# A decoder kernel whose first attention scores take k from SBUF instead of from a DRAM scratch, with two buffer changes in the second mixer and a 192-byte column buffer

## The chip, the core and the metric

The kernel runs on one core of a Trainium2 chip. The metric is the device time of one execution in microseconds (us), taken as the median of several runs. The engines are PE (TensorE, matmuls), DVE (VectorE), ACT (ScalarE), POOL (GpSimd) and SP (SyncE, which here issues DMAs). Matmul operands are float32 values split in a high and a low part, so each product is three matmul passes (L342 to L344), and every split costs one ACT cast (the high part) and one DVE subtraction (the low part).

## The reference, cut

A two-layer decoder on 512 tokens of width 1024, 16 heads of 64. Layer 0 has block-sparse (MoBA) attention between two SwiGLU blocks, layer 1 a dilated sliding-window attention with three branches that reads shared keys and values.

```python
for layer in range(DEPTH):
    if layer == N_A_LAYERS:                       # shared keys and values of three branches
        kv_bands = shared_kv_bands(modulate(rms_norm(x, kv_norm_g), ...), kv_w, cos, sin)
    x = x + 0.5 * gate0 * swiglu(modulate(rms_norm(x, g0), ...), w_gate, w_up, w_down)
    h = modulate(rms_norm(x, g1), ...)
    y = moba_mixer(h, w_qkv, w_o, cos, sin) if layer < N_A_LAYERS else dilated_mixer(h, w_q, w_o, kv_bands, cos, sin)
    x = x + gate1 * y
    x = x + 0.5 * gate2 * swiglu(modulate(rms_norm(x, g2), ...), w_gate, w_up, w_down)
return rms_norm(x, final_g)
```

Both mixers rotate q and k by position (`apply_rope`) before the scores.

## The kernel before

The residual stream `x`, the normed input `h_hi`/`h_lo` and two slots of weights (`w_raw`, `w_hi`, `w_lo`) lie in SBUF for the whole program. The program is a chain of phases: ffn0, mixA, woA, ffn1, kv, ffn2, mixB, woB, ffn3. Weights come in units of 512 KB that alternate between the two slots: SP loads a unit (`w_dma`, L327), ACT casts it (L333), DVE subtracts (L337), PE multiplies. The order on each engine is written out by hand, engine by engine, and semaphores tie the engines together; no scheduler moves anything.

**A mixer.** The 16 heads are worked in four groups of four. Group g's projections (pairs of 128 columns: in mixA pair 0 is q, pair 1 is k, pair 2 is v; in mixB pairs 0 to 2 are the q of the three branches) run while group g-1 is attended. Group 0 has nothing to hide behind. A pair of results goes from PSUM through DVE (`rope_multiply` L1430, or `late_read` L1017 for the very first pair) and POOL (`rope_add`, L1442 and L1446) into `rotated`; ACT casts it into a staging buffer (`rot_high`, L1454), DVE subtracts (`rot_low`, L1459), and POOL stores the 1 MB in a DRAM scratch (`rot_store`, L1466). `rope_add` holds all four heads of a group in rows of 32 per head and half. SP reads one head at a time back into the layout that the scores need (`load_k`, `load_q`, L1623; `load_v`, L1651): eight DMAs of 64 KB for a head's k in mixA, four for its q.

**What sets the order around the change.** SP's queue is in order. In group 0 of mixA it does: q of head 0 (waits for q's store), k of head 0 (waits for k's store), weight unit 9, v of head 0 (waits for v's store), weight unit 10, then k of head 1 (waits for the first score), unit 11, q of head 1, v of head 1. PE does units 0 to 9 of its weights in part, and then `score(a, s)` (L738, L739): steps s = 0 to 3 belong to head 0, step 4 begins head 1. `weigh_v` (L767, L768) is the product with v, two steps behind.

**Staging buffers.** `rot_st` is the one staging buffer; only the first pair of a mixer uses another one, `rot_late`, which lies on rows 3 to 6 of `att`. So in mixB, group 0, the cast of pair 2 into `rot_st` waits until the store of pair 1 out of `rot_st` has landed (`q_stored`). Behind that cast stands ACT's cast of weight unit 8, and behind DVE's `rot_low` of pair 2 stands the subtraction of unit 8. The third branch of the first head is copied straight from the staging buffer to `q_st` (L1665, four DMAs of 64 KB between SBUF rows), and the first score waits for these (`q_direct`).

**PSUM banks in mixB.** One unit is one tile of 128 columns and one bank. Group 0 uses the banks `FIRST_BANKS = (0, 1, 2, 3, 1, 7)` for its six tiles, later groups bank `unit % 3`. Tile 4 of group 0 lies in bank 1, and so tile 1 of group 1 (the program's unit 7, in bank 1) has to wait until DVE has read pair 2 of group 0 out.

Of the kernel before, what the change touches and what calls it, by code (L numbers as in the profile page):

```python
# [26 lines left out]
F32 = mybir.dt.float32  # L27
# [114 lines left out]
LATE_ROWS = (6, 7)  # L142
FIRST_BANKS = (0, 1, 2, 3, 1, 7)


def build(nc, x_t, c_col, ada_first, ada, ada_bias, gains, gate_up, down, mixa_w, kv_w, mixb_w, cos_t, sin_t,
          mask_a, mask_b, ident_in, out):
    with ExitStack() as ctx:  # L148
# [28 lines left out]
        shift_hl = sb(ctx, "shift_hl", [P, KT, 2], F32R)  # L177
        shift_out = sb(ctx, "shift_out", [P, 16])[:, 0:2]
        idle = sb(ctx, "idle", [P, S], BF16)
# [487 lines left out]
        def pe_mixer(pe, name):  # L667
# [9 lines left out]
            def substep(g, n):  # L677


                pair, k = n // KT, n % KT  # L680
                unit = n // 4
                first = isinstance(g, int) and g == 0
                follows = first and n < 2 * KT
                if n % 4 == 0:
                    pe.wait_ge(w_lo_done[unit % 2], g * 6 + u0 + unit - unit % 2 + 2)
                if is_a:
                    bank = mixa_bank(g, pair)
                    if k == 0:

                        pe.wait_ge(pair_free, g * 3 + p0 + pair + 1)  # L690
                    if follows:
                        pe.wait_ge(h_lo_done, h0 + k + 1)
                    if pair == 2:
                        mm = pe_k_tile_v(bank, unit % 2, k % 4, k, KT - 1)
                    else:
                        mm = pe_k_tile(bank, unit % 2, k % 4, h_hi, h_lo, k, KT - 1)
                else:
                    if n % 4 == 0:


                        pe.wait_ge(pair_free, g * 3 + p0 + pair + (1 if unit in (0, 2, 4) or first else 2))
                        if first and unit == 5:
                            pe.wait_ge(mod_ready, ADA_BLOCKS)
                    for j in range(2):
                        kt = 2 * (n % 4) + j
                        cols = slice(kt * P, (kt + 1) * P)
                        if follows:
                            pe.wait_ge(h_lo_done, h0 + kt + 1)
                        mm = three_passes(ps[:, FIRST_BANKS[unit] if first else unit % 3, :], w_hi[:, unit % 2, cols],
                                          w_lo[:, unit % 2, cols], h_hi[:, kt, :], h_lo[:, kt, :],  # L710
                                          kt == 0, kt == KT - 1)
                if n % 4 == 3:
                    mm.then_inc(unit_used, 1)
                elif n > 20 - 1 and not is_a and isinstance(g, int) and g == G - 1:
                    mm.then_inc(h_read, 1)
# [703 lines left out]

        rot_late = att[:, 3:7, :].bitcast(F32R).rearrange("p (a h) t -> p a h t", a=2)  # L1420

# [26 lines left out]

        def rot_high(act, n, busy, busy_n, late=False):

            act.wait_ge(rope_done, n * 2 + 2)
            if busy is not None:
                act.wait_ge(busy, busy_n)
            nc.scalar.copy((rot_late if late else rot_st[:])[:, 0], rotated[:]).then_inc(rot_hi_done, 1)  # L1454

        def rot_low(dve, n, late=False):
            st = rot_late if late else rot_st[:]
            dve.wait_ge(rot_hi_done, n + 1)
            nc.vector.tensor_tensor(st[:, 1], rotated[:], st[:, 0].bitcast(F32),  # L1459
                                    ALU.subtract).then_inc(rot_lo_done, 1)  # L1460

        def rot_store(pool, n, dst, dst_sem, late=False):
            st = rot_late if late else rot_st[:]
            pool.wait_ge(rot_lo_done, n + 1)
# [172 lines left out]

        def load_k(sp, layer, a, j):
            if j == 0:
                sp.wait_ge(k_stored, (a + 1) * 16 if layer == "A" else 16 * 16)  # L1640
# [13 lines left out]
        def load_q(sp, layer, a, j):  # L1654
            if layer == "B" and j == 0:
# [6 lines left out]
                for part in range(2):  # L1662
                    for half in range(2):
                        row = 64 * part + 32 * half
                        sp.dma_start(q_st[row:row + 32, 0, 2, :].bitcast(F32),  # L1665
                                     rot_st[0:32, part, half, :].bitcast(F32)).then_inc(q_direct, 16)
                return
# [69 lines left out]
        def act_mixer(act, name):  # L1737
# [5 lines left out]
            def rot(g, pair):  # L1743
                first = isinstance(g, int) and g == 0
                if first and pair < 2:
                    rot_high(act, rope0 + pair, None, 0, pair == 0)
                    return
                if is_a:
                    n, busy, busy_n = g * 2 + pair, (k_stored, q_stored)[pair], g * 16 + 16 * pair
# [171 lines left out]
        def dve_mixer(dve, name, g_block, col_n, stored):  # L1921
# [53 lines left out]
            def group(g, a, gemm, attend, early):  # L1975
# [4 lines left out]
                if not attend:  # L1980
                    for pair in range(3):
                        if pair == 0:
# [7 lines left out]
                            split(5)  # L1990
                            rot_low(dve, rot_n(g, 0), True)
                            continue
# [6 lines left out]
                        if pair == 1 or not is_a:  # L1999
                            rot_low(dve, rot_n(g, pair))  # L2000
                    split(8)
# [52 lines left out]
        def pool_mixer(pool, name):  # L2054
# [4 lines left out]
            def group(g, last=False):  # L2059
                for pair in range(3):  # L2060
# [10 lines left out]
                    if not is_a:  # L2071
                        if pair == 2:
                            pool.wait_ge(q_direct, g * 64 + 64)
                        rot_store(pool, n, dram_q["B"][g, pair], q_stored, pair == 0 and isinstance(g, int) and g == 0)
                    elif pair == 0:
                        rot_store(pool, n, dram_q["A"][g, 0], q_stored, isinstance(g, int) and g == 0)
                    else:
# [285 lines left out]
```

## Time and profile before

| | |
|---|---|
| median of 3 runs | 2497.1 us (2494.9 to 2497.17) |
| the profiled execution | 2495.63 us, span 2493.9 us |
| PE busy | 2448.9 us (98%) |
| DVE, ACT, POOL busy | 1376.2, 869.2 and 141.7 us |
| mean granted PE clock | 0.996 |
| mixA from its first scores | about 463 to 640 us |
| mixB from its first scores | about 1773 to 2100 us |

Times below are us from the start of the span. In the views an engine's idle time stands in brackets before the instruction that ended it, with what released it. The view by windows gives the granted PE clock of a stretch as a share of full speed (0.50 is 1.2 GHz, 1.00 is 2.4 GHz) and the busy share of the DMA engines. "To landing" is the time from a DMA's issue to the arrival of its last byte.

### The profile page before, as it was taken

What the parts mean: (1) busy time and instruction counts of PE and PEld (TensorE: products, weight loads), DVE (VectorE), ACT (ScalarE), POOL (GpSimd) and SP (SyncE); (2) the same over time, 40 slices, a digit from 0 to 9 for tenths busy, and PEclk for the clock granted to TensorE, in tenths of its full rate; (3) what the DMA queues carried; (4) which work ended last, traced back from release to release, by engine and by line L of the source; (5) the groups of instructions that cost most, each with busy time, mean ns of one, the idle gap of its engine ahead of it and who ended that gap; (6) DMA issues with size and microseconds to landing.
All of it is one profiled execution on the core that took longest, in us unless ns stands there. A gap on an engine that the chain in (4) does not pass through costs nothing. (4 is left out here: it accounts for less than half of the span.)

```text
span 2493.9 us, 33238 instructions
## 1 busy us (share of the span) xinstructions
PE 2448.9 (98%) x11992; PEld 2024.9 (81%) x11997; DVE 1376.2 (55%) x2105; ACT 869.2 (35%) x1230; POOL 141.7 (6%) x128
## 2 busy tenths in 40 slices
PE   9999999999999999999999999999999999999998
PEld 6888888888778888888888888888888887888886
DVE  7555446677675554465544555446667667433333
ACT  3222224345443332233333333223444444333321
POOL 0000000212000000011211000000211110000000
PEclk9999999999999999999999999999999999999999
DMA  6656532655446654335557666435887973222332
GB/s 245 196 188 194 163 118 92 209 192 179 139 155 191 192 179 133 103 114 207 179 183 246 188 189 192 132 118 143 249 223 214 241 218 97 92 93 93 101 93 84
DMA packets 135715, 408.79 MB, mean 164 GB/s; under 512 B 17088, under 2 KB 17472, under 8 KB 135616
## 3 DMA queue, kind: packets, MB, share of 16 engines
q1 hardware_dynamic: 122560, 357.16, 47.1%
q0 software_dynamic: 13056, 50.33, 5.2%
q8 instruction: 60, 0.98, 0.2%
q14 instruction: 39, 0.32, 0.0%
HBM read 353.95 MB, written 52.43 MB: 163 GB/s over the span
## 5 line engine op out<-in xcount | busy, mean ns | idle before, releaser
L337 DVE TENSOR_TENSOR w_lo<-w_raw,w_hi 128x1024 fp32r<-128x1024 f32 (+2 forms) x386 | 469.9, 1218 | 615.5 <-ACT w_hi L333 615.2
L342 PE MATMUL ps<-h_hi,w_hi 128*128 128x512 f32 x1872 | 745.3, 398 | 8.9 <-DVE w_lo L337 4.1
L344 PE MATMUL ps<-h_hi,w_lo 128*128 128x512 f32 x1872 | 732.2, 391 | 0.0
L343 PE MATMUL ps<-h_lo,w_hi 128*128 128x512 f32 x1872 | 730.9, 390 | 0.0
L333 ACT CAST w_hi<-w_raw 128x1024 fp32r<-128x1024 f32 (+2 forms) x388 | 395.5, 1019 | 765.5 <-PE ps L344 753.5
L342 PEld LDWEIGHTS ps<-h_hi,w_hi 128*128 128x128 f32 x1872 | 353.1, 189 | 83.7 <-DVE w_lo L337 8.9
L344 PEld LDWEIGHTS ps<-h_hi,w_lo 128*128 128x128 f32 x1872 | 352.4, 188 | 75.4
L343 PEld LDWEIGHTS ps<-h_lo,w_hi 128*128 128x128 f32 x1872 | 353.3, 189 | 67.1 <-issue 0.2
L342 PE MATMUL ps<-act_hi,w_hi 128*128 128x512 f32 x704 | 278.8, 396 | 0.2 <-DVE w_lo L337 0.2
L344 PE MATMUL ps<-act_hi,w_lo 128*128 128x512 f32 x704 | 277.8, 395 | 0.0
L343 PE MATMUL ps<-act_lo,w_hi 128*128 128x512 f32 x704 | 277.8, 395 | 0.0
L1328 DVE TENSOR_TENSOR prod<-ps,silu_g 128x512 f32<-128x512 f32 x86 | 59.5, 692 | 259.2 <-ACT silu_g L1286 259.2
L886 DVE SCALAR_TENSOR_TENSOR ada_acc<-ada_raw,c_act,ada_acc 128x1024 f32<-128x1024 f32 x126 | 161.2, 1279 | 0.7
L342 PEld LDWEIGHTS ps<-act_hi,w_hi 128*128 128x128 f32 x704 | 132.5, 188 | 34.1 <-issue 3.6
L344 PEld LDWEIGHTS ps<-act_hi,w_lo 128*128 128x128 f32 x704 | 132.5, 188 | 31.1
L343 PEld LDWEIGHTS ps<-act_lo,w_hi 128*128 128x128 f32 x704 | 132.6, 188 | 30.7
L1766 ACT CAST pt_hi<-ps 128x768 fp32r<-128x768 f32 (+4 forms) x128 | 78.5, 614 | 216.1 <-PE ps L748 215.9
L1286 ACT ACTIVATE silu_g<-ps 128x512 f32<-128x512 f32 x86 | 51.6, 600 | 252.3 <-PE ps L344 252.0
L1956 DVE TENSOR_TENSOR pt_lo<-ps,pt_hi 128x768 fp32r<-128x768 f32 (+4 forms) x128 | 92.4, 722 | 81.9 <-ACT pt_hi L1766 80.9
L767 PE MATMUL ps<-v_st,pt_hi 128*128 128x128 f32 x544 | 129.8, 278 | 5.9 <-DVE o_rows L1950 5.9
L768 PE MATMUL ps<-v_st,pt_lo 128*128 128x128 f32 x544 | 128.1, 275 | 0.0
L1442 POOL TENSOR_TENSOR rotated<-tmp 128x512 f32<-128x512 f32 x32 | 44.7, 1398 | 1446.5 <-DVE tmp L1017 1240.6
(162 smaller groups left out, 2808.1 us busy)
## 6 DMA issues: line engine op xcount, KB each, us to landing
w_raw<-gate_up SPq DMA_DIRECT2D x176, 512.0 KB, 3.7
ada_raw<-ada SPq DMA_DIRECT2D x144, 512.0 KB, 4.5
w_raw<-down SPq DMA_DIRECT2D x80, 512.0 KB, 3.6
w_raw<-kv_w SPq DMA_DIRECT2D x48, 512.0 KB, 3.6
w_raw<-mixa_w SPq DMA_DIRECT2D x34, 512.0 KB, 3.9
w_raw<-mixb_w SPq DMA_DIRECT2D x34, 512.0 KB, 5.6
kb<-rot_st POOLq DMA_DIRECT2D x12, 1024.0 KB, 5.0
k_hi<-kb SPq DMA_DIRECT2D x64, 192.0 KB, 4.8
```

The lines of the kernel that those rows point to most:

```text
L333: nc.scalar.copy(w_hi[:, slot, 0:n], w_raw[:, slot, 0:n]).then_inc(w_hi_done, 1)
L337: eng.tensor_tensor(w_lo[:, slot, 0:n], w_raw[:, slot, 0:n], w_hi[:, slot, 0:n].bitcast(F32), ALU.subtract).then_inc(w_lo_done[slot], 2)
L342: nc.tensor.matmul(out_ap, l_hi, r_hi, start=start, stop=False, skip_group_check=skip)
L343: nc.tensor.matmul(out_ap, l_hi, r_lo, start=False, stop=False, skip_group_check=skip)
L344: return nc.tensor.matmul(out_ap, l_lo, r_hi, start=False, stop=stop, skip_group_check=skip)
L767: nc.tensor.matmul(o_ps, pt_hi[:, s % 2, cols], v_both, start=n == 0, stop=False)
L768: mm = nc.tensor.matmul(o_ps, pt_lo[:, s % 2, cols], v_both, start=False, stop=n == n_last)
L886: nc.vector.scalar_tensor_tensor(out=ada_acc[:], in0=ada_raw[:, slot, :], scalar=c_act[:, k:k + 1], in1=ada_acc[:], op0=ALU.mult, op1=ALU. ...
L1286: nc.scalar.activation(silu_g[:, b, :], ps[:, 2 * b, :], ACT.Silu).then_inc(silu_done, 1)
L1328: nc.vector.tensor_tensor(prod[:, b, :], ps[:, 2 * b + 1, :], silu_g[:, b, :], ALU.mult).then_inc(pair_free, 1)
L1766: nc.scalar.copy(pt_hi[:, s % 2, 0:w], pt_ps[:, 0:w]).then_inc(pt_hi_done, 1)
L1956: nc.vector.tensor_tensor(pt_lo[:, s % 2, 0:w], pt_ps[:, 0:w], pt_hi[:, s % 2, 0:w].bitcast(F32), ALU.subtract).then_inc(pt_lo_done, 1)
```

## The change

Three edits, and a fourth of one number.

1. **mixA, head 0 of group 0: k on chip.** `load_k` for this head no longer waits for k's store in DRAM but for `rot_lo_done`, and copies the same eight pieces from rows 0 to 31 of `rot_st`. The store to DRAM stays, since heads 1 to 3 are read from it. ACT's next write of `rot_st` (group 1, pair 0) waits in addition for the eight copies.
2. **mixB, pair 2 of group 0** is staged in `att` rows 0 to 3 (`ROT_LATE = (0, None, 1)`), pair 0 in `att` rows 4 to 7 instead of 3 to 6. The cast of pair 2 doesn't wait for `q_stored` any more.
3. **mixB, tile 4 of group 0** goes to bank 4, after the row of factors that lay there has been copied (`rb_kept_done`). Tile 1 of group 1 waits for pair 1 of group 0 to be read out and no longer for pair 2.
4. `shift_out` takes 192 bytes of each partition instead of 64. Every buffer allocated behind it (those of the FFN, kv and mixer phases: `act_hi`, `act_lo`, `rot_st`, `k_hi`, `att` and so on) moves up by 128 bytes: `act_hi` starts at byte 106624 instead of 106496. `x`, `h_hi`, `h_lo` and the weight slots stay.

```diff
-FIRST_BANKS = (0, 1, 2, 3, 1, 7)
+FIRST_BANKS = (0, 1, 2, 3, 4, 7)
+ROT_LATE = (0, None, 1)
...
-        shift_out = sb(ctx, "shift_out", [P, 16])[:, 0:2]
+        shift_out = sb(ctx, "shift_out", [P, 48])[:, 0:2]
...
+                second = isinstance(g, int) and g == 1 and n < KT
...
-                        pe.wait_ge(pair_free, g * 3 + p0 + pair + (1 if unit in (0, 2, 4) or first else 2))
+                        pe.wait_ge(pair_free, g * 3 + p0 + pair + (1 if unit in (0, 2, 4) or first or second else 2))
+                        if first and unit == 4:
+                            pe.wait_ge(rb_kept_done, LATE.index("mixB") + 1)
...
-        rot_late = att[:, 3:7, :].bitcast(F32R).rearrange("p (a h) t -> p a h t", a=2)
+        def rot_buffer(late):
+
+            if late is None:
+                return rot_st[:]
+            return att[:, 4 - 4 * late:8 - 4 * late, :].bitcast(F32R).rearrange("p (a h) t -> p a h t", a=2)
...
         def load_k(sp, layer, a, j):
+            if layer == "A" and isinstance(a, int) and a == 0 and j == 0:
+
+                sp.wait_ge(rot_lo_done, rope_before("mixA") // 2 + 2)
+                for copy in range(2):
+                    for part, tile in enumerate((k_hi, k_lo)):
+                        for half in range(2):
+                            row = 64 * copy + 32 * half
+                            sp.dma_start(tile[row:row + 32, 0, 0, :].bitcast(F32),
+                                         rot_st[0:32, part, half, :].bitcast(F32)).then_inc(k_landed, 16)
+                return
...
-                if first and pair < 2:
-                    rot_high(act, rope0 + pair, None, 0, pair == 0)
+                if first and pair < 2 or first and not is_a:
+                    rot_high(act, rope0 + pair, None, 0, ROT_LATE[pair])
                     return
+                if is_a and isinstance(g, int) and g == 1 and pair == 0:
+                    act.wait_ge(k_landed, 128)
```

**SP in mixA, group 0**, from the last weight unit before the scores to the k of head 1. Before:

```order
L1623 DMA q_st<-qa 32x512 [waits q_stored]
L1623 DMA q_st<-qa 32x512 x3
L1623 DMA k_hi<-ka 32x512 [waits k_stored]
L1623 DMA k_hi<-ka 32x512
L1623 DMA k_lo<-ka 32x512 x2
L1623 DMA k_hi<-ka 32x512 x2
L1623 DMA k_lo<-ka 32x512 x2
L327 DMA w_raw<-mixa_w 128x1024 [waits w_lo_done1]
L1651 DMA v_st<-va 128x512 [waits v_stored]
L327 DMA w_raw<-mixa_w 128x1024 [waits w_lo_done0]
L1623 DMA k_hi<-ka 32x512 [waits s_done]
```

and now:

```order
L1631 DMA q_st<-qa 32x512 [waits q_stored]
L1631 DMA q_st<-qa 32x512 x3
L1654 DMA k_hi<-rot_st 32x512 [waits rot_lo_done]
L1654 DMA k_hi<-rot_st 32x512
L1654 DMA k_lo<-rot_st 32x512 x2
L1654 DMA k_hi<-rot_st 32x512 x2
L1654 DMA k_lo<-rot_st 32x512 x2
L328 DMA w_raw<-mixa_w 128x1024 [waits w_lo_done1]
L1669 DMA v_st<-va 128x512 [waits v_stored]
L328 DMA w_raw<-mixa_w 128x1024 [waits w_lo_done0]
L1631 DMA k_hi<-ka 32x512 [waits s_done]
```

The eight pieces keep their place in the queue; their source and the semaphore of the first of them are other ones.

**ACT in mixB, group 0**, the casts of pairs 0, 1 and 2 with the weight units between them. Before:

```order
L1454 CAST att<-rotated 128x1024 [waits rope_done]
L333 CAST w_hi<-w_raw 128x1024 [waits unit_used,w_landed0]
L1454 CAST rot_st<-rotated 128x1024 [waits rope_done]
L333 CAST w_hi<-w_raw 128x1024 [waits unit_used,w_landed1]
L1454 CAST rot_st<-rotated 128x1024 [waits q_stored,rope_done]
L333 CAST w_hi<-w_raw 128x1024 [waits unit_used,w_landed0]
```

and now:

```order
L1462 CAST att<-rotated 128x1024 [waits rope_done]
L334 CAST w_hi<-w_raw 128x1024 [waits unit_used,w_landed0]
L1462 CAST rot_st<-rotated 128x1024 [waits rope_done]
L334 CAST w_hi<-w_raw 128x1024 [waits unit_used,w_landed1]
L1462 CAST att<-rotated 128x1024 [waits rope_done]
L334 CAST w_hi<-w_raw 128x1024 [waits unit_used,w_landed0]
```

The third cast of rotated rows writes `att` and has lost the wait for the store. On no engine has an instruction been added, taken away or moved past another.

## Rows read from the trace of the kernel before

**Rows 1.** Waits of PE over the whole span: us in total, times, longest
```profile
PE ps L738 <- DMA k_lo<-ka: 4.4, 1, 4.4
```
**Rows 2.** Timeline of PE in mixA: start us, us, instruction, idle before
```profile
458.13 0.39 PE L344 MATMUL ps<-h_hi,w_lo 128*128 128x512 f32 x1
462.88 0.47 PE L738 MATMUL ps<-k_hi,q_st 128*128 128x128 f32 x1 [4.36 <-DMA k_lo<-ka]
...
472.29 0.22 PE L767 MATMUL ps<-v_st,pt_hi 128*128 128x128 f32 x1
...
476.49 0.27 PE L738 MATMUL ps<-k_hi,q_st 128*128 128x128 f32 x1
```
**Rows 3.** Windows: us, busy (x) of PE, PEld, DVE, ACT, POOL, PEclk, DMA share, GB/s
```profile
461.70:468.60 6.90, 5.72 (x16) 4.66 (x17) 1.87 (x5) 1.54 (x3) 1.99 (x2) 0.51 0.85 265
632.40:635.90 3.50, 3.50 (x10) 2.46 (x10) 2.17 (x6) 2.33 (x5) 0.00 (x0) 0.51 0.53 143
1766.00:1773.00 7.00, 4.61 (x20) 3.31 (x19) 4.75 (x6) 3.28 (x3) 0.00 (x0) 1.00 0.45 122
```
**Rows 4.** Timelines of DVE, POOL and SP's queue in mixA, group 0
```profile
449.76 1.23 DVE L1459 TENSOR_TENSOR rot_st<-rotated,rot_st 128x1024 fp32r<-128x1024 f32 x1 [3.52 <-ACT rot_st L1454]
...
451.60 0.77 POOL L1466 DMA_DIRECT2D ka<-rot_st  x1 [2.95 <-DVE rot_st L1459]
453.92 0.75 POOL L1492 DMA_DIRECT2D va<-v_out  x1 [1.56 <-DVE v_out L1484]
...
448.36 1.73 SPq L1623 DMA_DIRECT2D q_st<-qa  x4
457.83 0.78 SPq L1623 DMA_DIRECT2D k_hi<-ka  x2
...
461.92 0.42 SPq L1651 DMA_DIRECT2D v_st<-va  x1
...
463.60 0.82 SPq L1623 DMA_DIRECT2D k_hi<-ka  x2
...
468.85 1.82 SPq L1623 DMA_DIRECT2D q_st<-qa  x4
```
**Rows 5.** DMA issues (KB each, us to landing) and landing of L1665's copies
```profile
va<-v_out POOLq DMA_DIRECT2D x1, 1024.0 KB, 6.4
...
q_st<-qa SPq DMA_DIRECT2D x2, 64.0 KB, 2.9
...
DMA to landing us min/median/max: 2.0/3.2/3.8
```
**Rows 6.** DMA queue q0 from 453 to 455 us: packets, MB, share of 16 engines
```profile
q0 software_dynamic: 196, 0.80, 98.7%
```
**Rows 7.** Timeline of PE in mixB, group 1's tiles 1 and 2, first score
```profile
1762.03 0.47 PE L342 MATMUL ps<-h_hi,w_hi 128*128 128x512 f32 x1 [1.61 <-DVE tmp L1430]
...
1770.14 0.50 PE L342 MATMUL ps<-h_hi,w_hi 128*128 128x512 f32 x1 [2.39 <-DVE w_lo L337]
...
1773.02 0.47 PE L738 MATMUL ps<-k_hi,q_st 128*128 128x512 f32 x1
```
**Rows 8.** Timelines of DVE, POOL, ACT and SP's queue there; a DMA issue at 1752.3
```profile
1758.27 1.22 DVE L337 TENSOR_TENSOR w_lo<-w_raw,w_hi 128x1024 fp32r<-128x1024 f32 x1 [1.26 <-ACT w_hi L333]
...
1763.22 1.29 POOL L1446 TENSOR_TENSOR rotated<-tmp 128x512 f32<-128x512 f32 x1
...
1766.65 1.05 ACT L1454 CAST rot_st<-rotated 128x1024 fp32r<-128x1024 f32 x1 [8.48 <-DMA qb<-rot_st]
...
1766.59 1.74 SPq L1623 DMA_DIRECT2D q_st<-qb  x4
1768.98 2.50 SPq L1665 DMA_DIRECT2D q_st<-rot_st  x4
...
w_raw<-mixb_w SPq DMA_DIRECT2D x1, 512.0 KB, 11.4
```
**Rows 9.** The page's costliest groups: busy, mean ns, idle before
```profile
L342 PE MATMUL ps<-h_hi,w_hi 128*128 128x512 f32 x1872 | 745.3, 398 | 8.9 <-DVE w_lo L337 4.1
...
L342 PE MATMUL ps<-act_hi,w_hi 128*128 128x512 f32 x704 | 278.8, 396 | 0.2 <-DVE w_lo L337 0.2
```

More of the change, by code:

```diff
@@ L1447, in rope_add, with rot_high @@
                                     ALU.add).then_inc(rope_done, 1)
-        def rot_high(act, n, busy, busy_n, late=False):
+        def rot_high(act, n, busy, busy_n, late=None):
             act.wait_ge(rope_done, n * 2 + 2)
@@ L1453, in rot_high, with rot_low @@
                 act.wait_ge(busy, busy_n)
-            nc.scalar.copy((rot_late if late else rot_st[:])[:, 0], rotated[:]).then_inc(rot_hi_done, 1)
-        def rot_low(dve, n, late=False):
-            st = rot_late if late else rot_st[:]
+            nc.scalar.copy(rot_buffer(late)[:, 0], rotated[:]).then_inc(rot_hi_done, 1)
+        def rot_low(dve, n, late=None):
+            st = rot_buffer(late)
             dve.wait_ge(rot_hi_done, n + 1)
@@ L1460, in rot_low, with rot_store @@
                                     ALU.subtract).then_inc(rot_lo_done, 1)
-        def rot_store(pool, n, dst, dst_sem, late=False):
-            st = rot_late if late else rot_st[:]
+        def rot_store(pool, n, dst, dst_sem, late=None):
+            st = rot_buffer(late)
             pool.wait_ge(rot_lo_done, n + 1)
@@ L1664, in load_q @@
                         row = 64 * part + 32 * half
+                        src = rot_buffer(ROT_LATE[2] if isinstance(a, int) and a == 0 else None)
                         sp.dma_start(q_st[row:row + 32, 0, 2, :].bitcast(F32),
-                                     rot_st[0:32, part, half, :].bitcast(F32)).then_inc(q_direct, 16)
+                                     src[0:32, part, half, :].bitcast(F32)).then_inc(q_direct, 16)
                 return
@@ L1990, in group @@
                             split(5)
-                            rot_low(dve, rot_n(g, 0), True)
+                            rot_low(dve, rot_n(g, 0), ROT_LATE[0])
                             continue
@@ L1999, in group @@
                         if pair == 1 or not is_a:
-                            rot_low(dve, rot_n(g, pair))
+                            rot_low(dve, rot_n(g, pair), ROT_LATE[pair])
                     split(8)
@@ L2073, in group @@
                             pool.wait_ge(q_direct, g * 64 + 64)
-                        rot_store(pool, n, dram_q["B"][g, pair], q_stored, pair == 0 and isinstance(g, int) and g == 0)
+                        rot_store(pool, n, dram_q["B"][g, pair], q_stored,
+                                  ROT_LATE[pair] if isinstance(g, int) and g == 0 else None)
                     elif pair == 0:
-                        rot_store(pool, n, dram_q["A"][g, 0], q_stored, isinstance(g, int) and g == 0)
+                        rot_store(pool, n, dram_q["A"][g, 0], q_stored,
+                                  ROT_LATE[0] if isinstance(g, int) and g == 0 else None)
                     else:
```

## The prediction

> **What bounds the kernel now.** I read the list of PE's waits first. PE is busy nearly everywhere, so only its gaps, and stretches in which it is granted half its clock, can be won. The largest single wait is the first score of mixA, for k to come back from DRAM [rows 1]. PE's timeline puts it in place: the last matmul before it ends at 458.13 + 0.39 = 458.5, the score starts at 462.88 [rows 2]. The windows then show that the gap costs more than its length: from 461.7 to 468.6 the granted clock is 0.51, the lower level of 1.2 GHz, with 5.72 us of PE work in it, which at the full clock is half as long, 2.8 us less [rows 3]. In mixB two gaps stand before the first score: 1.61 us for DVE's reading of pair 2 and 2.39 us for weight unit 8 [rows 7]. I then read the queues that feed these places, SP's above all [rows 4, 8], because a wait that goes only helps until the next thing that is late.
>
> **Edit 1, k on chip.** Removed: the way through DRAM. DVE ends `rot_low` of k at 449.76 + 1.23 = 451.0, SP has issued q by 448.36 + 1.73 = 450.1, yet k's first load goes out at 457.83, when the store has landed [rows 4]. Now the first copy goes out at 451.0. The nearest price of such a copy is L1665's, the same size from the same buffer: four take 2.50 us to issue, 0.63 us each [rows 8]. The eighth starts at 451.0 + 7 x 0.63 = 455.4. These copies land in 2.0 to 3.8 us, median 3.2 [rows 5]; since the two stores fill the DMA engines just then (98.7%, rows 6) I take the median: 458.6, bounds 457.4 and 459.2. PE is ready at 458.5. So the wait falls from 4.4 to 0.1 us (0 to 0.7), a gain of 4.3 us, and with no gap the 2.8 us of clock come back too: 7.1 us at the first steps.
>
> **What is late next.** The SP queue. Behind k stand unit 9, then v of head 0, which waits for v's store. Before, that store landed at 453.92 + 6.4 = 460.3 [rows 4, 5], and SP came to v only at 461.92, so nobody waited. Now SP is there at 456.5 and waits. The store itself gets later: 0.5 MB of copies and the 0.5 MB of unit 9 now move while both stores are under way. At the rate of [rows 6], 0.80 MB in 2 us, this 1 MB is worth 2.5 us of all engines; the first two copies find them free, so I take 2.0: v's store lands at 462.3, bounds 460.3 (no delay) and 462.8. The Trainium skill says the same of the mechanism (DMA: Bandwidth & Descriptors, Issuing engines are not separate DMA queues): DMAs of SP and POOL interleave on the same 16 DMA engines.
>
> From 462.3 the queue runs on: v and unit 10 take 0.9, k of head 1 starts at 463.2 (before 463.60) and takes 3.6 us as before, unit 11 takes 0.4, q of head 1 starts at 467.2 (before 468.85), its last piece 1.4 later, and lands 2.9 us after that [rows 4, 5]: 471.5. PE wants it for the first score of head 1, before at 476.49, now 7.1 earlier, 469.4. It waits 2.1 us. The gain left is 476.49 - 471.5 = 5.0 us; 4.5 with the store at 462.8, and the full 7.0 with the store undelayed. v for the first `weigh_v` (472.29, now 465.2) is on the same delay and its wait lies inside this one. Behind that score SP waits for PE again and all that follows keeps its distance.
>
> One correction for the median. How long the clock stays low varies: the other low stretch behind a gap, 632.4 to 635.9, holds 3.50 us of work and so costs 1.75 us, not 2.8 [rows 3]. Runs whose stretch is shorter have less to win; I take off 0.5 (0 to 1.1). Edit 1 gives 4.5 us (3.4 to 7.0). ACT's new wait for the copies stands in group 1, when they have long landed: nothing.
>
> **Edits 2 and 3, mixB.** PE leaves unit 6 at 1762.03 - 1.61 = 1760.4. Unit 7 is split by 1758.27 + 1.22 = 1759.5 [rows 8], so with bank 1 free PE goes on: 1.6 us earlier, unit 7 ends at 1766.0 instead of 1767.7. For unit 8: POOL has the rotated rows at 1763.22 + 1.29 = 1764.5, ACT casts them at 1764.6 instead of 1766.65, 2.05 us earlier [rows 8]; the weights are there (1752.3 + 11.4 = 1763.7). The chain behind it (ACT's cast of unit 8, DVE's two subtractions) is unchanged, so PE starts unit 8 at 1770.14 - 2.05 = 1768.1, and wants the first score at 1773.02 - 2.05 = 1771.0. But the score needs L1665's four copies too. SP can't issue them before it has issued the q loads, which still wait for pair 1's store (1766.59 + 1.74 = 1768.3) [rows 8]. So the copies start at 1768.35 instead of 1768.98, and the score at about 1773.02 - 0.65 = 1772.4. Of the 4.0 us of gaps 0.65 is gained: 2.0 stay as a gap between units 7 and 8, from 1766.0 to 1768.1, and 1.4 become a new wait of the score for the copies. Bounds: 0, if another queue holds it, and 2.05, if the copies before were long landed when PE came. I take 0.7. The wait for `rb_kept_done` at tile 4 is free: the release of pair 0, for which tile 4 waited already, comes from DVE behind the same semaphore.
>
> **Edit 4** moves buffers by 128 bytes. `h_hi` lies today where `act_hi` will lie relative to multiples of 256 bytes (both 128 above), and matmuls reading either take 398 and 396 ns [rows 9]: nothing. The Trainium skill has a rule against it (DMA: Bandwidth & Descriptors, How a descriptor splits into AXI transactions): a descriptor that doesn't start at a multiple of 256 bytes pays extra beats, by its table 68 instead of 64 for 2 KB read from the staging buffers. That estimate is 6% of a 1 MB store, 0.15 us, twice before v's store has landed; the gain would be 4.9 instead of 5.2. No row here shows it.
>
> **Sum.** 4.5 + 0.7 = 5.2 us. The profiled execution has 2495.63 us with its 1.7 us outside the span, the runs' median 2497.1. I take the gain from the median: 2491.9.
>
> **The rivals.**
> *The SP queue isn't late.* The copies go through idle slots and v's store lands at 460.3. Then the clock and the gap are won whole: 7.1 - 0.5 + 0.7 = 7.3, giving 2489.8. For it: the engines are free from 451 to 453. Against: 98.7% afterwards. Chance 0.20.
> *The copies are late themselves.* With the stores' packets between theirs they land 2.5 us after PE is ready, at 461.0, and the gap is still long enough for the low clock. Only 1.9 + 0.7 = 2.6 is won: 2494.5. For it: no L1665 copy has run beside a full store. Against: their worst landing, 3.8. This is also the case in which the change doesn't do what it says, since the wait keeps its place and changes its name. Chance 0.18.
> *The clock falls in mixB.* The new gaps, 2.1 us before unit 8 and 1.4 before the score, lie close together, 3.5 idle in the 6.4 us from 1766.0; before, the clock stayed at 1.00 there with 4.61 us of 7 busy [rows 3]. If it falls it costs 1.75, as at 632: 2493.7. Chance 0.07.
> *Slower: the shifted buffers.* If the place of `act_hi` and `act_lo` matters to PE, 3 x 704 matmuls pay; from 2.5 ns each (5.2 us over 2112) this eats the gain, and at 5 ns, 10.6 us, the kernel ends at 2502.5. Against: [rows 9]. Chance 0.05.
>
> **How the numbers follow.** The forecast has 0.50, with its own range 2490.0 to 2493.2. A measurement of this kernel tells 0.2% (5.0 us) from no change, and the forecast lies just beyond it: 0.30 of its 0.50 and 0.19 of the first rival are faster, 0.49. Same: 0.20 of the forecast, 0.01 of the first rival, and the second and third, 0.46. Slower: 0.05. The range 2488.5 to 2495.6 leaves out the slower rival, the end of the first and of the second: under 0.2.
>
> **What would show it.** Right: PE's wait for k at 458 below 1 us and no low clock around 465; a new wait of the first score of head 1 for q (or k) of about 2 us near 470; SP's v load right behind v's store, after 461; in mixB no wait of unit 7, the cast of pair 2 right behind POOL, a wait of 1 to 2 us of the first score for the copies from `att`. Wrong: a wait over 2 us still at the first score, v's load before 461, or a matmul on `act_hi` whose mean moved from 396 ns.

## The result, and the profile after

The changed kernel takes **2477.2 us** (median of 4 runs, 2476.22 to 2478.88) against 2496.12 us before (median of 4, 2494.9 to 2497.17). The ratio is 0.9921, 95% interval 0.9905 to 0.9937: 0.8% faster. Two later sets of runs gave 2475.69 and 2477.84 us, ratios 0.9911 [0.9896, 0.9926] and 0.9917 [0.9903, 0.993]. The gain is 18.9 us. The prediction had 5.2 us and a range whose fast end was 2488.5: it was wrong, and the kernel gained most by the one edit that the prediction had priced at nothing.

The profiled execution took 2478.88 us, with a span of 2477.2 (before 2495.63 and 2493.9). Its waits of TensorE over the whole span come first (us in total, times, longest us):

```profile
PE ps L771 <- DVE o_rows L1971: 5.8, 12, 1.3
PE ps L343 <- DVE w_lo L338: 5.0, 8, 2.0
...
PE ps L742 <- DMA k_lo<-rot_st: 3.3, 1, 3.3
...
PE ps L742 <- DMA q_st<-att: 1.6, 1, 1.6
```

The 4.4 us for k [rows 1] have become 3.3, with a new source and in the same place. That is 1.1 us of 18.9, so the waits don't hold the answer. The page's groups do. These two stood in the page of before (busy us, mean ns of one | idle before), next to the first passes of [rows 9]:

```profile
L344 PE MATMUL ps<-h_hi,w_lo 128*128 128x512 f32 x1872 | 732.2, 391 | 0.0
...
L344 PE MATMUL ps<-act_hi,w_lo 128*128 128x512 f32 x704 | 277.8, 395 | 0.0
```

And this is the page of after:

```profile
L343 PE MATMUL ps<-h_hi,w_hi 128*128 128x512 f32 x1872 | 746.0, 398 | 6.0 <-DVE w_lo L338 3.7
L345 PE MATMUL ps<-h_hi,w_lo 128*128 128x512 f32 x1872 | 733.0, 392 | 0.0
...
L343 PE MATMUL ps<-act_hi,w_hi 128*128 128x512 f32 x704 | 275.3, 391 | 0.3 <-DVE w_lo L338 0.2
L345 PE MATMUL ps<-act_hi,w_lo 128*128 128x512 f32 x704 | 274.2, 389 | 0.0
L344 PE MATMUL ps<-act_lo,w_hi 128*128 128x512 f32 x704 | 274.0, 389 | 0.0
```

Every matmul that reads `act_hi` or `act_lo` has become 5 to 6 ns shorter, and none that reads `h_hi`. The key and value projections show the same, with the normed input (`kv_h_lo`) as the stationary operand in the first of these groups and (`kv_h_hi`) as the moving one in the second; before, both groups were at 394 ns. After, from the groups by shape:

```profile
L345 PE MATMUL ps<-w_hi,kv_h_lo 128*128 128x512 f32 x192 | 74.7, 389 | 0.0
...
L345 PE MATMUL ps<-kv_h_hi,w_lo 128*128 128x512 f32 x176 | 68.5, 389 | 0.0
```

A matmul's record overlaps the next one's, so the time that the path gets is in the distance from start to start. TensorE's timeline of before, two passes of the same kind in a stretch without a gap, 60 matmuls apart (start us, us, instruction):

```profile
2356.61 0.39 PE L342 MATMUL ps<-act_hi,w_hi 128*128 128x512 f32 x1
...
2370.61 0.39 PE L342 MATMUL ps<-act_hi,w_hi 128*128 128x512 f32 x1
```

The same of after, again 60 apart:

```profile
2342.00 0.39 PE L343 MATMUL ps<-act_hi,w_hi 128*128 128x512 f32 x1
...
2355.60 0.39 PE L343 MATMUL ps<-act_hi,w_hi 128*128 128x512 f32 x1
```

14.00 us over 60 is 233.3 ns, 13.60 over 60 is 226.7. The difference of 6.7 ns, times 3 x 704 matmuls on `act_hi` and `act_lo` and 3 x (192 + 176) on `kv_h_hi` and `kv_h_lo`, 3216 in all, would be 21 us. In before the distance isn't the same everywhere: most stretches have 232.3 to 232.5 ns, as this one does, again 60 matmuls apart and 13.95 us long:

```profile
2400.71 0.39 PE L342 MATMUL ps<-act_hi,w_hi 128*128 128x512 f32 x1
...
2414.66 0.39 PE L342 MATMUL ps<-act_hi,w_hi 128*128 128x512 f32 x1
```

With 232.5 it is 5.8 ns and 19 us. Whether anything of the 5.2 us forecast for the waits and the clock is in the measured 18.9 can't be read from this; the experiments take it apart.

### The profile page after: what moved, and what is told of

It reads as the page before. It is cut to its first block and busy times, and to the rows that moved or that the text cites. A ratio compares the mean times of both kernels' runs of the same rounds, so it can differ in the third digit from the quotient of the medians.

```text
span 2477.2 us, 33242 instructions
## 1 busy us (share of the span) xinstructions
PE 2436.5 (98%) x11997; PEld 2026.3 (82%) x11997; DVE 1377.9 (56%) x2105; ACT 868.7 (35%) x1230; POOL 141.5 (6%) x128
## 3 DMA queue, kind: packets, MB, share of 16 engines
q0 software_dynamic: 13056, 50.33, 5.7%
```

## The experiments: what edit 4 does

My theory after the result: edit 4 is nearly the whole gain, because a matmul runs faster when its stationary and its moving operand begin at the **same offset from a multiple of 256 bytes**. In the built kernels, x, `h_hi`, `h_lo`, `w_hi` and `w_lo` begin 128 bytes behind such a multiple. `act_hi` begins at 106496 (0 behind one) before and at 106624 (128 behind) after, `kv_h_hi` at 143360 and 143488. All tiles inside these tensors are multiples of 256 bytes long, so one offset holds for a whole tensor. The rivals: that only the phase buffers' own place counts, or that edits 1 to 3 did it.

The first four kernels ran together; before took 2499.39 us beside them (19 runs). **Edit 4 alone** on the kernel before:

```diff
-        shift_out = sb(ctx, "shift_out", [P, 16])[:, 0:2]
+        shift_out = sb(ctx, "shift_out", [P, 48])[:, 0:2]
```

> The kernel before with edit 4 alone: shift_out takes 192 bytes, everything behind it moves up by 128. Placement theory: the gain is in the pace of the matmuls that read act_hi, act_lo, kv_h_hi or kv_h_lo. Those four passes fall from a mean of 394 to 396 ns to about 389 to 391, 3216 matmuls x 6 ns = 19 us: about 2477 us. Gap theory (the gain is in the gaps before the first scores): no change, 2496, and means as before.

2477.65 us, ratio 0.9917 [0.9901, 0.9934]. Passes on `act_hi` 391 and 389 ns, on `h_hi` 398 and 391. The whole of the gain is there with not one instruction moved. **All but edit 4**:

```diff
-        shift_out = sb(ctx, "shift_out", [P, 48])[:, 0:2]
+        shift_out = sb(ctx, "shift_out", [P, 16])[:, 0:2]
```

> The changed kernel without edit 4: shift_out back at 64 bytes, edits 1 to 3 kept. Placement theory: 2493 to 2497 us, the means of the act and kv_h passes back at 394 to 396 ns. Gap theory: it keeps the gain, 2477 to 2479. It also measures what edits 1 to 3 bring by themselves; from the two traces I expect 0 to 3 us (the wait for k is 3.3 instead of 4.4, the two gaps of mixB 3.7 instead of 4.0, and the low clock falls differently).

2494.49 us, ratio 0.998 [0.9971, 0.999]: edits 1 to 3 by themselves bring 4.9 us, more than the 0 to 3 expected here and about what was forecast for the whole change. The group by shape of this kernel:

```profile
L345 PE MATMUL ps<-act_hi,w_lo 128*128 128x512 f32 x704 | 277.9, 395 | 0.0
```

**Everything at 0.** The changed kernel, with 128 bytes ahead of x, so that both operands begin at multiples of 256. The phase buffers are then back at an offset of 0, where they were slow before:

```diff
+        sb(ctx, "pad", [P, 32])
         x = sb(ctx, "x", [P, KT, S])
```

> The changed kernel with 128 unused bytes put ahead of x, so that x, h, the weight slots and all phase buffers start at multiples of 256 bytes. Two forms of the placement theory. Same place: a matmul is fast when its two SBUF operands start at the same offset within 256 bytes; then all stay fast, 2477 us. Own place: a buffer that starts 128 above a multiple of 256 is fast by itself and one at the multiple is slow; then all 8800 big matmuls are slow, h's too, 2477 + 8800 x 6 ns = about 2530 us.

2477.89 us, ratio 0.9914 [0.9897, 0.993]. **Only the phase buffers 256 bytes on**, so at an offset of 0 against the weights' 128:

```diff
-        shift_out = sb(ctx, "shift_out", [P, 48])[:, 0:2]
+        shift_out = sb(ctx, "shift_out", [P, 80])[:, 0:2]
```

> The changed kernel with shift_out at 320 bytes: the phase buffers lie 256 bytes above their place in the kernel before, so again at multiples of 256 while the weights are 128 above one. Both forms of the placement theory: slow again, act means 394 to 396 ns, about 2494 us. If instead only the old place (multiples of 2048) is bad, it stays fast: 2477.

2495.46 us, ratio 0.9984 [0.9974, 0.9994]: nothing is left of the shift's gain. First the group of the kernel with everything at 0, then that of the one with 256 bytes:

```profile
L346 PE MATMUL ps<-act_hi,w_lo 128*128 128x512 f32 x704 | 274.1, 389 | 0.0
```

```profile
L345 PE MATMUL ps<-act_hi,w_lo 128*128 128x512 f32 x704 | 278.1, 395 | 0.0
```

An offset of 0 is slow beside weights at 128 and fast beside weights at 0. `act_hi` begins at the same byte in both kernels, 106752; only what is allocated ahead of the phase buffers (x, h, the weights) lies 128 bytes apart. The buffers' own place is out as a cause.

**How wide is the rule?** Three kernels change only the size of `shift_out` (448, 128 and 96 bytes in place of 192), and one more takes 224:

> The changed kernel with shift_out of 448 bytes: the phase buffers lie 384 bytes behind their old place, at the weights' offset modulo 256 but not modulo 512. If equal offsets modulo 256 are enough, the passes on act_hi and kv_h are 389 ns and the span near 2475 us; if it takes 512 or more, 395 ns and near 2493 us.

> The changed kernel with shift_out of 128 bytes: phase buffers 64 bytes behind their old place, so 64 bytes (modulo 256) from the weights' offset. If any difference of offsets costs alike: 395 ns and 2493 us. If the cost grows with the distance, 391 to 393 ns. If 64 is as good as equal, 389 ns.

> The changed kernel with shift_out of 96 bytes: phase buffers 32 bytes behind their old place, 96 bytes (modulo 256) from the weights' offset. If any difference costs alike: 395 ns and 2493 us; if the cost depends on the distance, between the values of 64 and of 128 bytes.

> The changed kernel with shift_out of 224 bytes: phase buffers at 160 modulo 256, the weights at 128, a difference of only 32 bytes. If any difference costs alike: 395 to 396 ns on act_hi, 2493 us. If a small one is cheap: 389 to 392 ns, 2475 to 2484 us.

One run each, beside 2497.97 us of before (2498.64 for the last):

| `shift_out`, bytes | phase buffers' offset | difference from the weights' | `act_hi,w_lo`, ns | time, us |
|---|---|---|---|---|
| 448 | 128 | 0 (256 by multiples of 512) | 389 | 2476.34 |
| 128 | 64 | 64 | 395 | 2494.56 |
| 96 | 32 | 96 | 396 | 2498.14 |
| 224 | 160 | 32 | 395 | 2497.45 |

It is 256 bytes, not 512 (the first row). There is no middle ground in the means: a difference of 32 bytes costs as much as one of 128. The times are of single runs and say no more than which side a kernel is on.

**The pair the other way round.** Pads put x, h and the weights at 0 and the phase buffers at 128 (the place that was fast after the change):

```diff
+        sb(ctx, "pad", [P, 32])
         x = sb(ctx, "x", [P, KT, S])
...
-        shift_out = sb(ctx, "shift_out", [P, 48])[:, 0:2]
+        shift_out = sb(ctx, "shift_out", [P, 16])[:, 0:2]
```

> The changed kernel with a pad of 128 bytes ahead of x and shift_out back at 64 bytes: x, h and the weights lie at 0 modulo 256, and the phase buffers at 128. If what matters is that both operands of a matmul have the same offset: h passes fast (390 to 391 ns), act_hi and kv_h passes slow (395), span near 2491 us. If the place of the phase buffers alone mattered (128 good, 0 bad), they would be fast here, span near 2474 us.

2491.52 us, with `act_hi,w_lo` at 395 ns and `h_hi,w_lo` at 391, and with `act_hi` at byte 106624, where the changed kernel has it at 389. And, as the sharpest test, the rule should also make the **h passes** slow, which no kernel so far had done. A pad between `h_lo` and the weights leaves h at 128 and puts the weights and the phase buffers at 0:

```diff
         h_lo = sb(ctx, "h_lo", [P, KT, S], F32R)
+        sb(ctx, "pad", [P, 32])
         w_raw = sb(ctx, "w_raw", [P, 2, UNIT])
```

> The changed kernel with a pad of 128 bytes between h_lo and w_raw: x, h_hi and h_lo stay at 128 modulo 256, the weights and all phase buffers go to 0. If the pair of operands decides: act_hi and kv_h passes stay at 389 ns, the 5616 matmuls on h go from 391 to 395 to 397 ns each, 5616 x 4 to 6 ns = 22 to 34 us, a time near 2500 to 2510 us. If h is always fast (the place or size of the phase buffers alone matters): 391 ns and 2476 us.

2501.9 us, against 2476.34 of the kernel with 448 bytes (one run each, in different sets): 25.6 us lost over 5616 matmuls, 4.6 ns each. The groups by shape of this kernel:

```profile
L344 PE MATMUL ps<-h_hi,w_hi 128*128 128x512 f32 x1872 | 753.6, 403 | 6.7 <-DVE w_lo L339 4.5
...
L346 PE MATMUL ps<-h_hi,w_lo 128*128 128x512 f32 x1872 | 740.3, 395 | 0.0
...
L346 PE MATMUL ps<-act_hi,w_lo 128*128 128x512 f32 x704 | 274.1, 389 | 0.0
...
L346 PE MATMUL ps<-w_hi,h_lo 128*128 128x256 f32 x128 | 36.1, 282 | 0.0
```

The two have changed places: h at 395, `act_hi` at 389. Its timeline has 14.00 us over 60 passes on h, the 233.3 ns again:

```profile
2340.50 0.39 PE L344 MATMUL ps<-h_hi,w_hi 128*128 128x512 f32 x1
...
2354.50 0.39 PE L344 MATMUL ps<-h_hi,w_hi 128*128 128x512 f32 x1
```

That the equality of both offsets modulo 256 sets the pace of the 512-column matmuls is shown from both sides. The last row of the groups sets a bound: the passes on h with 256 columns (v's projection in mixA) have unequal offsets here too, and their means are 286, 282 and 281 ns, against 287, 282 and 282 in before, where the offsets are equal. They didn't get slower. What in the chip makes it so is open; no run here looks inside a matmul.

**The price of the same 128 bytes elsewhere.** The shift also moves the staging buffers of the stores off the multiples of 256. The DMA table of the page, the row of POOL's queue: first before, then after (packets, MB, share of 16 engines):

```profile
q0 software_dynamic: 13056, 50.33, 5.2%
```

```profile
q0 software_dynamic: 13056, 50.33, 5.7%
```

The share is 5.2 or 5.3% in every kernel whose phase buffers begin at a multiple of 256, and 5.6 or 5.7% in every other. The store `vb<-q_st` lands in 6.7 us in the first kind and in 7.2 to 7.3 in the second. To see whether that costs time I ran the kernel with everything at 0 and the changed one side by side, 5 runs each:

> The changed kernel with 128 bytes of pad ahead of x, as before in this study: all operands of the matmuls at 0 modulo 256, and the stores' staging buffers too. If the unaligned stores cost time in the changed kernel: 1 to 3 us faster than it, q0 at 5.2 to 5.3%. If they lie beside other work all the way: within 1 us of it. First values on another chip: 2477.89 us here, 2475.69 to 2477.2 us for the changed kernel.

> The changed kernel on the same chip as the run beside it; 0.991 to 0.992 of before, q0 at 5.7%, vb<-q_st 7.3 us.

2478.55 and 2477.84 us, with intervals of the ratio [0.9909, 0.9936] and [0.9903, 0.993]. It costs nothing that can be measured. That these stores lie beside other work would explain it, but isn't shown.

## The experiments: the waits

Four kernels on one chip, before at 2498.41 us. First the changed kernel itself, as a yardstick:

> The changed kernel once more, beside three variants of it on one chip. Its first four runs had a median of 2477.2 us, 0.9921 of before. Every theory expects a ratio of 0.991 to 0.993 here; the spread of its runs is the yardstick for the three others.

2475.69 us (2474.94 to 2479.26). Its own four runs lie 4.3 us apart, so a difference of 2 us is at the edge of what the next kernels can show. **Without edit 1**, head 0 loads k from DRAM again:

```diff
         def load_k(sp, layer, a, j):
-            if layer == "A" and isinstance(a, int) and a == 0 and j == 0:
...
-                return
             if j == 0:
...
-                if is_a and isinstance(g, int) and g == 1 and pair == 0:
-                    act.wait_ge(k_landed, 128)
```

> The changed kernel without its edit 1: head 0 of the first mixer loads k from DRAM again. Theory A (edit 1 shortens the first wait from 4.4 to 3.3 us, and the low clock behind it from 2.8 to 1.6 us): 2 to 3 us slower than the changed kernel, first-score wait 4.4 to 4.7 us. Theory B (the copies only exchange one wait for another, and what the three edits gained lies all in the second mixer): within 1 us of the changed kernel.

2479.18 us (2476.71 to 2481.75), the wait back at 4.5 us. **Without edits 2 and 3**, that is before with edits 1 and 4:

> The kernel before with edits 1 and 4 alone: the second mixer's third pair shares rot_st and tile 4 shares bank 1 again. Theory A (edits 2 and 3 brought the 2.0 us by which the wait on unit 7 and the first scores shrank, and a clock fall behind it took 1.7 of them back): within 2 us of the changed kernel, unit 7's wait of 2 to 3 us is back in the second mixer. Theory B (they brought their full forecast, 2 us and more): 2 to 4 us slower than the changed kernel.

2480.38 us (2477.85 to 2483.11); the waits in the second mixer are back at 1.6 us for unit 7 and 2.5 for unit 8. The medians say 3.5 us for edit 1 and 4.7 for edits 2 and 3, but the intervals of the ratios overlap ([0.9896, 0.9926], [0.9906, 0.9933], [0.991, 0.9938]), and edit 4 alone ran at 2477.65 in another set, 0.9917 of before, which is where the whole change lies too (0.9921, 0.9911 and 0.9917). So the three edits help where edit 4 is left out (4.9 us together); on top of edit 4 no gain of theirs is clear of the noise, and how it divides is not settled.

**Why edit 1 gave so little.** The timelines of after in the first mixer show TensorE, SP's queue and POOL:

```profile
456.44 0.39 PE L345 MATMUL ps<-h_hi,w_lo 128*128 128x512 f32 x1
460.14 0.33 PE L742 MATMUL ps<-k_hi,q_st 128*128 128x128 f32 x1 [3.31 <-DMA k_lo<-rot_st]
...
472.66 0.27 PE L742 MATMUL ps<-k_hi,q_st 128*128 128x128 f32 x1
```

```profile
449.31 1.24 SPq L1654 DMA_DIRECT2D k_hi<-rot_st  x2
450.59 1.96 SPq L1654 DMA_DIRECT2D k_lo<-rot_st  x2
452.59 2.63 SPq L1654 DMA_DIRECT2D k_hi<-rot_st  x2
455.27 3.13 SPq L1654 DMA_DIRECT2D k_lo<-rot_st  x2
458.44 0.58 SPq L328 DMA_DIRECT2D w_raw<-mixa_w  x1
459.48 0.35 SPq L1669 DMA_DIRECT2D v_st<-va  x1
```

```profile
449.89 0.77 POOL L1474 DMA_DIRECT2D ka<-rot_st  x1 [2.94 <-DVE rot_st L1467]
452.22 0.75 POOL L1500 DMA_DIRECT2D va<-v_out  x1 [1.56 <-DVE v_out L1492]
```

The first two copies are issued at the forecast pace, 0.62 us each. Once POOL's two stores are out, at 449.89 and 452.22, the issuing itself slows down, to 1.57 us each at the end, and the eight take 9.1 us. Their landing, 3.2 us in the row that I had taken, is in the view of this line, with the first and last start of the copies to `k_lo` above it:

```profile
L1654 SPq DMA_DIRECT2D k_lo<-rot_st x4: 592/1388/1634, 450.6 to 456.9; - x4
...
DMA to landing us min/median/max: 2.0/4.6/5.8
```

The copies in the middle take longest to land. The last one, on which the score waits, starts at 456.9 and is there at 460.1, 3.2 us later, as forecast. What is late is its start: 7.6 us after the first copy's, where the forecast had 4.4. That difference is the whole gap.

So k is there 3.3 us after TensorE is ready, and in this profile the gap still brings the low clock behind it. The window from 461 to 464 (us, busy of PE, PEld, DVE, ACT, POOL, PEclk, DMA share, GB/s):

```profile
461.00:464.00 3.00, 3.00 (x10) 2.41 (x9) 0.59 (x5) 1.54 (x3) 1.02 (x1) 0.50 0.81 302
```

Such a gap doesn't always do so: without edit 4, and with everything at 0, the wait was 3.1 us and the clock from 461 to 464 was 1.00.

If the stores are the cause, moving them should free the copies. Three kernels move them. The first sends va's store first and ka's only when the copies have landed:

```diff
+            if layer == "A" and isinstance(a, int) and a == 0 and j == 1:
+                sp.wait_ge(k_stored, 16)
...
                         v_store(pool, p, dram_v["A"][g, 0])
+                        if isinstance(g, int) and g == 0:
+                            pool.wait_ge(k_landed, 128)
+                            rot_store(pool, rope0 // 2 + 1, dram_k["A"][0, 0], k_stored)
...
-                    else:
+                    elif not (isinstance(g, int) and g == 0):
                         rot_store(pool, n, dram_k["A"][g, 0], k_stored)
```

> The changed kernel with the order of two stores of group 0 changed: va's goes ahead of ka's, and ka's waits until the eight on-chip copies of k have landed; head 1's load of k waits for that store by name. Theory A (the copies were slow, 9.1 us for eight issues and 3.3 us of wait on TensorE, because both 1 MB stores filled the DMA engines beside them): the eight issues take 5 to 7 us, the wait for k_lo<-rot_st falls from 3.3 to 0 to 2 us, 1.5 to 4 us faster than the changed kernel. Theory B (the copies are slow by their own form, 32 partitions of 64 KB, or the store of va alone is enough to fill the engines): the wait stays at 3 us or more and the time within 1 us. Theory C (the late store of ka delays head 1): a new wait of TensorE on k_lo<-ka or q_st<-qa near 472 us into the span, and no gain.

2482.2 us (2479.23 to 2485.96). Theory A's shorter wait came, and so did theory C's new one: the wait for the copies is 1.34 us and no low clock follows, but ka's store takes 8.0 us from 457.63, head 1's k is loaded from 465.62 on, its q behind that, and its first score waits 6.09 us, three times what was saved, with the clock at 0.50 from 474 to 478. TensorE's timeline of this kernel:

```profile
457.06 0.33 PE L742 MATMUL ps<-k_hi,q_st 128*128 128x128 f32 x1 [1.34 <-DMA k_lo<-rot_st]
...
474.44 0.45 PE L742 MATMUL ps<-k_hi,q_st 128*128 128x128 f32 x1 [6.09 <-issue]
```

The second only exchanges the order of the stores (with the same wait of SP for `k_stored`):

```diff
+                            rot_store(pool, rope0 // 2 + 1, dram_k["A"][0, 0], k_stored)
...
-                    else:
+                    elif not (isinstance(g, int) and g == 0):
                         rot_store(pool, n, dram_k["A"][g, 0], k_stored)
```

> The changed kernel with va's store ahead of ka's in group 0 of the first mixer (ka's goes out right behind it), and a named wait for ka's store ahead of head 1's load of k. If the stores beside the copies cause the wait of 3.3 us: the stores now begin near 451 us instead of 450, four or five copies are issued before them, the wait on k_lo<-rot_st is 1.3 to 2.5 us, head 1 starts without a wait, 1 to 3 us faster than the changed kernel. If head 1's k comes late: a wait of 1 us or more near 470 us and no gain.

2480.63 us (2480.16 to 2481.3), and a miss: the wait grew to 5.7 us. The stores went out at 451.12 and 451.89, right behind the fifth copy; that the last copies met both at once is the likely reason. The third holds both stores back until the eighth copy has been issued:

```diff
+                sp.sem_inc(k_copied, 1)
                 return
...
+                        if isinstance(g, int) and g == 0:
+                            pool.wait_ge(k_copied, 1)
                         rot_store(pool, n, dram_k["A"][g, 0], k_stored)
```

> The changed kernel with ka's and va's stores of group 0 held back until all eight copies have been issued. If the stores cause the slow copies: eight issues in 5 to 6 us instead of 9.1, the wait on k_lo<-rot_st 0 to 0.5 us, no low clock behind it; the stores leave near 454 us. Then either head 1 and the first P x V start in time, and the kernel is 3 to 4.5 us faster than the changed one, or v_st<-va or q of head 1 comes late, with a new wait near 466 to 472 us that takes 1 to 5 us back.

2480.61 us (2477.65 to 2482.79). The eight copies are issued in 6.0 us and land in 2.0 to 2.2 us at the median, and the wait for them is gone: the stores beside them made them slow, which this shows. One of the eight still took 1.53 us to issue, with no store out and the engines 0.34 busy from 450 to 454, so the stores aren't the only thing that slows an issue. The time isn't gained all the same. Its timeline of TensorE:

```profile
457.94 0.38 PE L743 MATMUL ps<-k_hi,q_st 128*128 128x256 f32 x1 [0.94 <-DVE negmax L1956]
465.89 0.45 PE L772 MATMUL ps<-v_st,pt_hi 128*128 128x128 f32 x1 [2.26 <-DMA v_st<-va]
472.88 0.30 PE L743 MATMUL ps<-k_hi,q_st 128*128 128x128 f32 x1 [0.99 <-issue]
```

The three gaps come to 4.2 us, against 3.3 in the changed kernel. The longest is now for v, 2.26 us, with 0.59 of the clock from 466 to 470. SP can load v only behind va's store, which now leaves at 455.10 instead of 452.22 and lands at about 462.95. The engines stood at 0.34 from 450 to 454 and at 0.99 from 458 to 462: holding the stores back put their megabytes later, and what depends on them came late. The Trainium skill says of the queues (DMA: Bandwidth & Descriptors, Issuing engines are not separate DMA queues) that SP's and POOL's DMAs interleave on the same 16 engines. The traces agree: SP's copies landed in 2.0 us at the median with POOL's stores held back, and in 4.6 beside them. The same section calls the time to issue a DMA usually small beside the DMA; here the issue of a 64 KB copy went from 0.62 to 1.57 us with the stores beside it. None of the three orders beats the changed kernel.

## Why the prediction was wrong

**The step that failed is edit 4.** It said that `h_hi` lay where `act_hi` would lie, that the first passes took 398 and 396 ns [rows 9], and so: nothing. Two things were wrong in it. The numbers compared weren't of the same kind: the first pass on h often begins behind a wait (8.9 us of idle stand in its row) or behind a matmul of another kind, and is then recorded as longer: 0.47 and 0.50 us in rows 7, 0.45 behind a score at 476.71 in before, where 0.39 is usual. Of such starts `act_hi` has hardly any. The second and third passes, which begin without any idle time, stood two lines further down in the same page, at 391 for h against 395 for `act_hi`. That was the gap of 4 ns, in the open. And the argument ran backwards: that h already had the offset that `act_hi` was to get was a reason to expect `act_hi` to become as fast as h, not a reason for no effect. 4 ns of mean over 3216 matmuls would have given 13 us; the distances from start to start give 19 to 21, and the kernels 17 (from 2494.49 without the shift to 2477.89 with everything at 0) to 22 (from 2499.39 to 2477.65). The rival on the shifted buffers was right that their place matters to TensorE, and had the wrong sign: 2.5 to 5 ns more, "slower", at 0.05. It counted the 2112 matmuls on `act_hi` and `act_lo` and left out the 1104 on `kv_h_hi` and `kv_h_lo`. "A matmul on `act_hi` whose mean moved from 396 ns" was named as what would show me wrong, and did.

**Edit 1** was mis-sized: a wait of 0.1 us forecast, 3.3 measured. The second rival describes what happened, copies landing 2.5 us after TensorE is ready and a gain of 1.9 us: they landed 3.3 us after, and the wait fell by 1.1. The term that failed is the issuing, 0.63 us a copy taken from copies with no full store beside them: here it went up to 1.63, and the last copy started 7.6 us after the first instead of 4.4. The 3.2 us for its landing held.

**What is late next** was half right. This part of the trace of after runs 1.7 us ahead of before (the last matmul before the scores starts at 456.44 instead of 458.13), so the forecast 462.3 for v's store is 460.6 here. v's load does go out right behind the store, at 459.48: the store landed at 452.22 + 7.2 = 459.4, 0.8 us later than by its old 6.4 and not 2.0. SP hardly waited for it, since the slow copies had kept it until 459.0. The forecast wait of head 1's first score for q didn't come: the score, at 472.66, starts with no wait [before 476.49, rows 2]. It had no cause left, since the first score was not 4.3 us earlier against its own loads. From the last matmul before the scores to head 1's first score it is 16.2 us now and was 18.4: 2.1 us gained in this execution, 4.5 forecast.

**Edits 2 and 3** went as forecast in their mechanism. Unit 7's wait is gone, unit 8 waits 2.02 us (forecast 2.0), and the first score 1.64 us for the copies from `att` (forecast 1.4). The gaps come to 3.7 us instead of 4.0, so 0.3 us is gained where 0.65 was forecast:

```profile
1752.32 0.50 PE L343 MATMUL ps<-h_hi,w_hi 128*128 128x512 f32 x1 [2.02 <-DVE w_lo L338]
...
1756.97 0.47 PE L742 MATMUL ps<-k_hi,q_st 128*128 128x512 f32 x1 [1.64 <-DMA q_st<-att]
```

The third rival came with it in this execution. The window behind the score:

```profile
1757.00:1761.30 4.30, 4.30 (x14) 3.52 (x15) 0.96 (x2) 1.96 (x3) 3.30 (x3) 0.61 0.86 326
```

0.39 of 4.30 us is 1.7 us lost, close to the 1.75 that the prediction had taken from the stretch at 632. It isn't in every execution: in the profile of the second set the same window has a clock of 1.00. Such stretches come and go by the run, which may be one reason why runs of one kernel lie 4 us apart.

**The sum of edits 1 to 3** came out at 4.9 us where 5.2 were forecast, from terms of which one was too high and none was known to be too low; that agreement should not be taken as support for the working.

## What to carry to other kernels

Look at where the operands of a matmul begin in SBUF. Here the two operands of a 512-column matmul had to be equal modulo 256 bytes to run at the full pace; the size of a small buffer allocated between them (64 bytes here) can break that and cost 2.5 to 3% of each such matmul, with no wait and no idle engine to show for it, only a mean that is 1% higher. When groups of the same shape differ by 1% in their mean, compare the passes that start without idle time, and take the difference seriously: multiplied by some thousands of instructions it is worth more than the largest wait. And before an on-chip copy replaces a way through DRAM, ask what else is on the DMA engines in those few microseconds: in the three orders tried here, removing one wait only brought the next.

## What the runs showed of the hardware

- In a stretch without gaps and at the full clock, a 128x128 by 128x512 matmul of 4-byte operands started every 226.7 ns when both began at the same offset modulo 256, and every 232.5 or 233.3 ns, by the stretch, when they didn't. The difference is all or nothing in the means (32, 64, 96 and 128 bytes alike, 395 to 396 ns against 389), and the same with the normed input as the moving or as the stationary operand. The Trainium skill (SBUF — State Buffer, Operand start alignment) asks of an operand only that it starts at a multiple of its element size. The section is about legality, not speed. All kernels here keep its rule, and these runs show that it isn't enough for the pace.
- Narrower matmuls didn't show it: with 256 columns, the passes on h kept 281 to 287 ns when their offsets became unequal, and with 128 columns `ident,probs` has 273 ns in before, where its offsets differ by 128, and 274 in after, where they are equal. `v_st,pt_hi` (278 ns in all) says nothing of it: both operands lie behind `shift_out` and keep equal offsets in every kernel.
- Stores from staging buffers that don't begin at a multiple of 256 bytes take more of the DMA engines: 5.6 to 5.7% against 5.2 to 5.3 for the same 50.33 MB, and 7.3 us against 6.7 for `vb<-q_st`. The prediction cited the rule for that (DMA: Bandwidth & Descriptors, How a descriptor splits into AXI transactions, of the Trainium skill) and said that no row showed it. The rows of after do: by the rounded shares of all kernels the stores take 6 to 10% more, by the landing time 7 to 9%, where the prediction's estimate was 6; no loss of time could be measured.
- SP's queue issued its 64 KB copies more slowly beside two 1 MB stores: eight took 9.1 us, up to 1.63 us each, against 6.0 us with the stores held back, where seven took about 0.6 us and one 1.53.
